# Squares of two tiles interleaved, samples scaled inside waits and half a product group moved ahead of the sample transposes, in the norms of a hybrid encoder step

## The chip, the cores and the metric

One core of a Trainium2 chip runs the whole kernel in one launch. The metric is device time in microseconds, the median of several runs.

## The reference

Two encoder layers over 256 prompt tokens (one sequence) and 8 x 16 sample tokens, 384 tokens in all, of width 1024. Every layer has three blocks, each closed by a gated residual, with RMSNorm before and after the block:

```
h = rms_norm(x, gains[0]) * (1 + sc1) + sh1
x = x + MACARON_W * ga1 * rms_norm(swiglu(h, w_f1_in, w_f1_out), gains[1])
h = rms_norm(x, gains[2]) * (1 + sc2) + sh2
y, rows = token_mixing(h, ...)
x = x + ga2 * rms_norm(y, gains[3])
h = rms_norm(x, gains[4]) * (1 + sc3) + sh3
x = x + MACARON_W * ga3 * rms_norm(swiglu(h, w_f2_in, w_f2_out), gains[5])
```

`rms_norm` divides a token's 1024 values by the root of their mean square plus 1e-6. Shift, scale and gate (`sh`, `sc`, `ga`) come from the condition of the sequence through `w_ada`, so all prompt tokens share theirs and every sample sequence has its own. Token mixing is one projection `h @ w_in` into three groups of heads (stick-breaking attention, gated linear attention, sparse attention with an indexer), joined by `w_out`. All is float32.

## The kernel before, in words

**Tiles.** The 384 tokens are three tiles of 128: the samples are tile 2, the prompt tiles 0 and 1. `TILES = (2, 0, 1)` is the order in which a norm takes them, so k = 0 is the samples, k = 1 is tile 0, k = 2 is tile 1. Between norms the activations lie transposed, feature by token, as `act_hi` and `act_lo` (the value split in a high part and a rest), eight chunks f of 128 features. Each weight unit of 128 x 2048 is loaded by SP, split by ACT (`w_hi`, the line of `split_hi`) and DVE (`w_lo`, L1282), and every product is three: hi x hi, lo x hi, hi x lo (L1926 to L1928 for projections into the block, L1973 to L1977 and L2007 to L2009 for projections back to tokens). Weights keep PE fed unit by unit; the first unit behind a norm is split ahead of it into `first_hi` and `first_lo`.

**A norm.** There are six, three a layer: `nth` 0 behind FFN 1, 1 behind the mixing, 2 behind FFN 2. The last one only updates x. In `last_two` PE ends the products of a projection tile by tile, the last unit half by half of the 1024 columns (`last_products`: six products of 512 columns for the left half, `y_left_done`, six for the right). For each tile ACT squares and sums the left and right half of y (`sum_y`: L920, L923, then Sqrt L927); DVE multiplies y with the gate (`gate_y`: mean L1371, left L1372, right L1374, reciprocal L1376) and updates x in two halves (L1379). Then the new x is normalised: ACT squares its halves (`sum_new_x`: L932, L935, Sqrt L939), DVE adds the left sum to eps for that Sqrt (`norm_new_x`: L1385), takes the reciprocal (L1387) and multiplies x by it in two halves (L1391, `x_left_normed`, `x_normed`). The order, written out by hand on both engines in `renorm`, is y0, x0, y1, y2, x1, x2.

**Back to features.** PE transposes the samples (`transpose_samples`, L1838) when the normalised samples are there, then does `last_products(2)` for tile 1, a group of products with `w_ada` (L1868, conditioning of later blocks, `ada_quarters`), the transposes of tile 0 and tile 1 (L1844), and, where `nth != 1`, a second group with `w_ada`. ACT applies scale and shift to the prompt chunks on their way out of PSUM (`modulate`: L914 to act_hi, L915 to y), DVE takes act_lo from them (`split_prompt`, L1305). The samples are handled by DVE alone: scale (L1250, whole width of 1024), shift (L1256), high part (L1298), low part (L1300) in `modulate_samples` and `split_samples`, and in front of FFN 2 (`nth` 1's norm) by halves of 512 columns (`scale_half` L1319, `shift_half` L1325, `high_half` L1330, `low_half` L1335). PE's first product of the next block (L1926) waits for act_lo of chunk 0, which stands behind these in DVE's queue.

**Key duplicates.** In the mixing, the 64 rows of the key of the sparse attention and of its indexer are needed on both halves of the partitions (`kc_dup`, `ki_dup`). PE makes them with `dup_eye`, a 64 x 128 matrix of two identities (L2130), ACT copies them from PSUM (L1017). The index products (L2152, L2153) read `ki_dup`.

Each engine runs its own instructions in the written order; semaphores tie them together. Loads of `w_ada` are issued by POOL when PE has used a slot, loads of other weights by SP when DVE has split a slot.

Of the kernel before, what the change touches and what calls it, by code (L numbers as in the profile page):

```python
# [26 lines left out]
P = 128  # L27
# [26 lines left out]
def encoder_program(nc, T):  # L54
# [93 lines left out]
    with ExitStack() as ctx:  # L148
# [37 lines left out]
        dup_eye = place("dup_eye", [P, P])  # L186
# [204 lines left out]
        dup_mm = sig("dup_mm", 2)  # L391
# [224 lines left out]
        def _(pool):  # L616
# [15 lines left out]
            for t, v in ((ones_v, 1.0 / DV), (causal, 0.0), (gla_mask, 1.0),  # L632
                         (restart, 1.0), (dup_eye, 0.0), (spread, 0.0), (sb_mask_c, 0.0), (head_rows, 0.0),
                         (other_seq, 0.0), (parity, 1.0), (ones_row, 1.0)):
                pool.memset(t[:], v)
# [9 lines left out]
            keep_where(dup_eye[0:64, :].rearrange("p (a n) -> p a n", a=2), [[0, 2], [-1, 64]], 0, 1, ALU.not_equal, 1.0)  # L645
# [194 lines left out]
        def _(act):  # L840
# [37 lines left out]
            for l in range(DEPTH):  # L878
# [38 lines left out]
                def sum_y(nth, k):  # L917
# [3 lines left out]
                                   accum_out=st(k, LEFT_SUM)).then_inc(y_left_squared.sem, 1)  # L921
                    wait_y(act, l, nth, k)
# [6 lines left out]
                def sum_new_x(nth, k):  # L929

                    act.wait_ge(x_left_ready.sem, x_left_ready.at(l, TT * nth + k + 1))
                    act.activation(square_out[:, 0:512], x[:, TILES[k], 0:512], ACT.Square, scale=float(D) ** -0.5,  # L932
                                   accum_out=st(k, X_LEFT_SUM)).then_inc(x_left_squared.sem, 1)
                    act.wait_ge(x_ready.sem, x_ready.at(l, TT * nth + k + 1))
# [6 lines left out]
                def renorm(nth):  # L941

                    if nth == 2 and l == LAST:
                        for k in range(TT):
                            sum_y(nth, k)
# [65 lines left out]
                def copy_kvi():  # L1011
# [191 lines left out]
        def _(dve):  # L1203
# [50 lines left out]
            def shift_samples(nth):  # L1254

                dve.tensor_tensor(samples_4d(own_tok[2]), samples_4d(own_tok[2]), per_seq(3 * (nth % 3)), ALU.add)  # L1256
                dve.drain()

# [19 lines left out]
            for l in range(DEPTH):  # L1278
# [10 lines left out]
                def modulate_samples(nth):  # L1289

                    if l > 0 or nth > 0:
                        scale_samples(3 * l + nth)
                    shift_samples(nth)

                def split_samples():

                    tok = own_tok[2].rearrange("p (f n) -> p f n", f=KD)
                    dve.tensor_copy(act_hi[:, :, NP:N], tok)  # L1298
                    dve.drain()
                    dve.tensor_tensor(act_lo[:, :, NP:N], tok, act_hi[:, :, NP:N].bitcast(F32), ALU.subtract)  # L1300

# [6 lines left out]
                def split_prompts(nth):  # L1308

                    for f in range(KD):  # L1310
                        split_prompt(nth, f)
# [26 lines left out]
                def split_all_by_halves(nth):  # L1338

                    shift_half(nth, 0)  # L1340
# [6 lines left out]
                    if nth == 0:  # L1347
# [1113 lines left out]
```

## Time and profile before

| | |
|---|---|
| timed, median of 3 runs | 1632.11 us (1631.75 to 1632.22) |
| the profiled execution | 1630.43 us, of which its span 1628.8 |
| PE busy | 1587.3 us (97%), 10214 matmuls |
| DVE busy | 814.3 us (50%) |
| ACT busy | 586.2 us (36%) |
| POOL busy | 151.7 us (9%) |
| mean granted TensorE clock | 0.994 of full speed |
| moved by DMA | 266.01 MB, mean 163 GB/s |

The span runs from the first to the last instruction of one execution. Busy shares are over all stages; for a norm one reads the timeline of that stretch: a row has the start (from the span's start), the duration, the engine, the line, the operation, output and inputs, the count, and in brackets how long the engine had been idle and what released it. Rows that merge several instructions have one start and the time of all of them. Instructions of one engine overlap by some hundredths of a microsecond to a few tenths, so distances between starts are the better measure of what one costs in a queue.

### The profile page before, as it was taken

Reading aid. Unit: us, or ns where it says so; the run is one execution under the profiler, and the core shown is the slowest. Engines: PE = TensorE matmul, PEld = TensorE weight load, DVE = VectorE, ACT = ScalarE, POOL = GpSimd, SP = SyncE. Lnnn points to the kernel's source line nnn. Section 1 sums busy time; section 2 is a strip of 40 time slices with the busy share of each in tenths; the row PEclk is TensorE's granted clock in tenths of the full one; section 3 lists DMA queues with packets and bytes.
Section 4 is the critical chain, followed back from the end, with each engine's and each line's share of the span. In section 5 each row is a group of like instructions: output and inputs, shape, how many; then the busy total and the mean of one; then the engine's idle time right before and its main releaser. Section 6 shows DMA issues by size and latency. Waiting matters only on the chain.

```text
span 1628.8 us, 26038 instructions
## 1 busy us (share of the span) xinstructions
PE 1587.3 (97%) x10214; PEld 1448.3 (89%) x10214; DVE 814.3 (50%) x1202; ACT 586.2 (36%) x816; POOL 151.7 (9%) x227
## 2 busy tenths in 40 slices
PE   5999999999999999999999999999999999999998
PEld 4999998879998799998879999987899879999987
DVE  3434442458658733443364444326675685444424
ACT  4322222363455522222262222224535644222222
POOL 5000000010242000000010000000105310000000
PEclk9999999999999999999999999999999999999999
DMA  9777744753345577444557744355534273444432
GB/s 346 232 232 214 233 128 155 229 147 104 104 134 191 148 233 231 123 121 152 185 176 228 233 129 129 129 181 181 143 106 128 83 233 104 128 125 119 135 119 84
DMA packets 254150, 266.01 MB, mean 163 GB/s; under 512 B 11727, under 2 KB 216653, under 8 KB 254066
## 3 DMA queue, kind: packets, MB, share of 16 engines
q1 hardware_dynamic: 231968, 183.52, 37.7%
q0 software_dynamic: 22080, 81.26, 14.4%
q8 instruction: 61, 1.00, 0.3%
q14 instruction: 23, 0.19, 0.0%
q10 hardware_dynamic: 18, 0.04, 0.0%
HBM read 258.70 MB, written 6.09 MB: 163 GB/s over the span
## 4 chain that ended last, share of the span: by engine, by line
PE 90%; DVE 5%; ACT 2%; DMA 1%; DVEq 1%; issue 1%; SPq 0%; ACTq 0%
PE ps L1926 20%; PE ps L1928 19%; PE ps L1927 19%; PE ps L1973 7%; PE ps L1975 7%; PE ps L1977 7%; PE ps L1868 2%; DMA w_ada_g<-in_w_ada_dram 1%; PE ps L2009 1%; PE ps L2007 1%; PE ps L2008 1%; DVE x L1379 1%; PE ps L1990 1%; PE ps L2264 0%; PE ps L2137 0%
## 5 line engine op out<-in xcount | busy, mean ns | idle before, releaser
L1926 PE MATMUL ps<-act_hi,w_hi 128*128 128x384 f32 x1696 | 572.6, 338 | 0.4 <-DVE w_lo L1282 0.4
L1928 PE MATMUL ps<-act_hi,w_lo 128*128 128x384 f32 x1696 | 567.1, 334 | 0.0
L1927 PE MATMUL ps<-act_lo,w_hi 128*128 128x384 f32 x1696 | 566.8, 334 | 0.0
L1282 DVE TENSOR_TENSOR w_lo<-w_raw,w_hi 128x2048 fp32r<-128x2048 f32 x158 | 363.7, 2302 | 238.2 <-ACT w_hi L898 207.6
L1926 PEld LDWEIGHTS ps<-act_hi,w_hi 128*128 128x128 f32 x1696 | 318.4, 188 | 10.8 <-issue 9.9
L898 ACT ACTIVATE w_hi<-w_raw 128x2048 fp32r<-128x2048 f32 x128 | 245.4, 1917 | 227.6 <-PE ps L1977 226.8
L1927 PEld LDWEIGHTS ps<-act_lo,w_hi 128*128 128x128 f32 x1696 | 318.5, 188 | 0.0
L1928 PEld LDWEIGHTS ps<-act_hi,w_lo 128*128 128x128 f32 x1696 | 318.3, 188 | 0.0
L962 ACT ACTIVATE silu_g<-ps 128x384 f32<-128x384 f32 x88 | 43.3, 492 | 546.7 <-PE ps L1928 546.7
L1422 DVE TENSOR_TENSOR hid_f<-silu_g,ps 128x384 f32<-128x384 f32 x88 | 48.8, 554 | 375.4 <-ACT silu_g L962 375.4
L1973 PE MATMUL ps<-w_hi,hid_hi 128*128 128x512 f32 x480 | 148.6, 391 | 0.0
L1975 PE MATMUL ps<-w_hi,hid_lo 128*128 128x512 f32 x480 | 147.9, 389 | 0.0
L1977 PE MATMUL ps<-w_lo,hid_hi 128*128 128x512 f32 x480 | 147.9, 389 | 0.0
L1977 PEld LDWEIGHTS ps<-w_lo,hid_hi 128*128 128x128 f32 x480 | 90.1, 188 | 18.9
L1975 PEld LDWEIGHTS ps<-w_hi,hid_lo 128*128 128x128 f32 x480 | 90.1, 188 | 18.9
L1973 PEld LDWEIGHTS ps<-w_hi,hid_hi 128*128 128x128 f32 x480 | 89.4, 188 | 17.9
L702 POOL DMA_DIRECT2D w_ada_g<-in_w_ada_dram x16 | 11.7, 734 | 495.8 <-PE ps L1977 495.8
L885 ACT ACTIVATE w_hi<-w_raw 128x2048 fp32r<-128x2048 f32 x30 | 57.5, 1915 | 0.0
L1428 DVE TENSOR_TENSOR hid_lo<-hid_f,hid_hi 128x384 f32 (+1 forms) x88 | 49.1, 558 | 10.9 <-issue 0.2
L712 POOL DMA_DIRECT2D w_ada_sb<-in_w_ada_dram x32 | 23.0, 719 | 263.3 <-PE ps L1868 259.1
L1868 PE MATMUL ps<-w_ada_sb,silu_cT 128*32 128x256 f32 x752 | 45.7, 382 | 0.0
L1519 DVE COPY U<-ps 128x384 f32<-128x384 f32 x24 | 13.4, 558 | 57.5 <-PE ps L1928 57.2
(421 smaller groups left out, 1555.1 us busy)
## 6 DMA issues: line engine op xcount, KB each, us to landing
w_raw<-in_w_ffn_in_dram SPq DMA_DIRECT2D x176, 512.0 KB, 5.1
w_ada_sb<-in_w_ada_dram POOLq DMA_DIRECT2D x45, 1024.0 KB, 7.1
w_raw<-in_w_ffn_out_dram SPq DMA_DIRECT2D x88, 512.0 KB, 4.1
w_raw<-in_w_in_dram SPq DMA_DIRECT2D x46, 512.0 KB, 4.7
w_ada_g<-in_w_ada_dram POOLq DMA_DIRECT2D x16, 1024.0 KB, 5.4
w_raw<-in_w_out_dram SPq DMA_DIRECT2D x16, 512.0 KB, 4.7
w_ada_g<-in_w_ada_dram SPq DMA_DIRECT2D x5, 1024.0 KB, 15.8
w_ada_s<-in_w_ada_dram POOLq DMA_DIRECT2D x3, 1024.0 KB, 10.9
```

The source lines that it names most:

```text
L885: act.activation(w_hi[slot][:], w_raw[slot][:], ACT.Copy).then_inc(hi_ready.sem, 1)
L898: act.activation(w_hi[slot][:], w_raw[slot][:], ACT.Copy).then_inc(hi_ready.sem, 1)
L1282: dve.tensor_tensor(w_lo[slot][:], w_raw[slot][:], w_hi[slot][:].bitcast(F32), ALU.subtract).then_inc(lo_ready.sem, 1)
L1422: dve.tensor_tensor(hid_f32[:], silu_g[:, s % 2, :], ps[:, IN_BANK[s % 2] + 1, 0:N], ALU.mult)
L1428: dve.tensor_tensor(hid_lo[:, chunk, :], one, hid_hi[:, chunk, :].bitcast(F32), ALU.subtract).then_inc(hidden_ready.sem, 1)
L1868: m = pe.matmul(ps[32 * g:32 * g + 32, bank, 0:256], silu_cT[:, 2 * q + k, :], w_ada_slot[slot][:, k, 256 * g:256 * g + 256], start=(q + k ...
L1926: pe.matmul(out, w, a, start=first, stop=False)
L1927: pe.matmul(out, w, al, start=False, stop=False)
L1928: return pe.matmul(out, wl, a, start=False, stop=last)
L1973: pe.matmul(y_half(tile, half), a, w_hi[slot][:, cols[half]], start=first, stop=False)
L1975: pe.matmul(y_half(tile, half), al, w_hi[slot][:, cols[half]], start=False, stop=False)
L1977: m = pe.matmul(y_half(tile, half), a, w_lo[slot][:, cols[half]], start=False, stop=last)
```

## The change

1. ACT's `sum_y` and `sum_new_x` are cut into `square_y_left`, `square_y_right`, `square_x_left`, `square_x_right`. For tiles 0 and 1 the order becomes y1, left y2, left x1, (drain), right y2, right x1, x2, with the left square of x1 written into the other half of `square_out`.
2. DVE's `gate_y` and `norm_new_x` are cut the same way; the order for the two prompt tiles becomes y1, left gate of y2, the left half of the samples' scale, right gate of y2, mean of x1, update of x by y2, normalise x1 left, mean of x2, x1 right, x2.
3. The samples are scaled, shifted and split by halves behind every norm (`split_by_halves`), the left half of the scale inside `renorm`, the right half at the start of `split_by_halves` (for `nth` 2 where it was).
4. On PE the left half of `last_products(2)` stands ahead of the sample transposes.
5. The key duplicates are copied by ACT from U, in two halves of 64 partitions each; `dup_eye`, its products and their semaphore go.

In the diff `split_first` holds what `split_all_by_halves(0)` did for the first block.

```diff
-                    sum_y(nth, 0)
-                    sum_new_x(nth, 0)
-                    sum_y(nth, 1)
-                    sum_y(nth, 2)
-                    sum_new_x(nth, 1)
-                    sum_new_x(nth, 2)
+                    square_y_left(nth, 0)
+                    square_y_right(nth, 0)
+                    square_x_left(nth, 0)
+                    square_x_right(nth, 0)
+                    square_y_left(nth, 1)
+                    square_y_right(nth, 1)
+                    square_y_left(nth, 2)
+                    square_x_left(nth, 1, square_out[:, 512:1024])
+                    act.drain()
+                    square_y_right(nth, 2)
+                    square_x_right(nth, 1)
+                    square_x_left(nth, 2)
+                    square_x_right(nth, 2)
...
-                    for n, dst in ((1, ki_dup), (0, kc_dup)):
-                        act.wait_ge(dup_mm.sem, dup_mm.at(l, n + 1))
-                        act.activation(dst[:], ps[:, 6 + n, 0:N], ACT.Copy).then_inc(dup_ready.sem, 1)
+                    for dst, tile in ((ki_dup, KI), (kc_dup, KV)):
+                        for rows in (slice(0, 64), slice(64, 128)):
+                            ins = act.activation(dst[rows, :], U[0:64, tile, :], ACT.Copy)
+                        ins.then_inc(dup_ready.sem, 1)
...
-                def scale_half(nth, a):
-
-                    dve.wait_ge(sample_tr.sem, sample_tr.at(0, 3 * l + nth))
+                def scale_half(norm, a):
+
+                    banks = SAMPLE_BANKS_F2 if norm % 3 == 2 else SAMPLE_BANKS
+                    dve.wait_ge(sample_tr.sem, sample_tr.at(0, norm))
                     four = lambda t: t.rearrange("p (f b t) -> p f b t", f=KD // 2, t=S)
-                    dve.tensor_tensor(four(half_tok(a)), four(ps[:, SAMPLE_BANKS_F2[a], :]), per_seq(3 * nth + 1)[:, half_of(a)], ALU.mult)
+                    dve.tensor_tensor(four(half_tok(a)), four(ps[:, banks[a], :]), per_seq(3 * (norm % 3) + 1)[:, half_of(a)], ALU.mult)
                     dve.drain()
...
+                def split_by_halves(nth):
+
+                    if nth != 2:
+                        scale_half(3 * l + nth, 1)
                     shift_half(nth, 0)
                     high_half(0)
                     low_half(0)
                     split_prompt(nth, 0)
                     if nth == 2:
-                        scale_half(nth, 1)
+                        scale_half(3 * l + nth, 1)
                     split_prompt(nth, 1)
...
                     gate_y(nth, 0)
-                    norm_new_x(nth, 0)
+                    new_x_mean(nth, 0)
+                    new_x_rstd(nth, 0)
+                    normalise(0, x_left_normed, left)
+                    normalise(0, x_normed, right)
                     gate_y(nth, 1)
-                    gate_y(nth, 2)
-                    norm_new_x(nth, 1)
-                    norm_new_x(nth, 2)
+                    gate_left(nth, 2)
+                    scale_half(3 * l + nth + 1, 0)
+                    gate_right(nth, 2)
+                    new_x_mean(nth, 1)
+                    add_y(nth, 2)
+                    new_x_rstd(nth, 1)
+                    normalise(1, x_left_normed, left)
+                    new_x_mean(nth, 2)
+                    normalise(1, x_normed, right)
+                    new_x_rstd(nth, 2)
+                    normalise(2, x_left_normed, left)
+                    normalise(2, x_normed, right)
...
-                    modulate_samples(0)
-                    split_samples()
-                    split_prompts(0)
+                    split_by_halves(0)
...
-                scale_half(2, 0)
-                split_all_by_halves(2)
+                split_by_halves(2)
...
-                    def last_products(k):
+                    def last_products(k, halves=range(2)):
                         tok, slot = slice(TILES[k] * P, (TILES[k] + 1) * P), (u + 1) % 2
-                        for half in range(2):
+                        for half in halves:
...
+                    last_products(2, (0,))
                     pe.wait_ge(gate_read.sem, gate_read.at(l, 2 * nth + 2))
                     banks = SAMPLE_BANKS_F2 if nth == 1 else SAMPLE_BANKS
                     pe.wait_ge(x_left_normed.sem, x_left_normed.at(l, TT * nth + 1))
                     transpose_samples(banks, range(4))
                     pe.wait_ge(x_normed.sem, x_normed.at(l, TT * nth + 1))
                     transpose_samples(banks, range(4, KD)).then_inc(sample_tr.sem, 1)
-                    last_products(2).then_inc(unit_used.sem, 1)
+                    last_products(2, (1,)).then_inc(unit_used.sem, 1)
...
-                    for n, tile in enumerate((KV, KI)):
-                        pe.matmul(ps[:, 6 + n, 0:N], dup_eye[0:64, :], U[0:64, tile, :], start=True, stop=True).then_inc(dup_mm.sem, 1)
```

## Rows read from the trace of the kernel before

**Rows 1.** PE's waits: who waited <- for whom: us, times, longest us

```profile
PE ps L1926 <- DVE act_lo L1305: 7.2, 6, 2.4
```

**Rows 2.** Timeline near 330 us, PE: start us, us, engine, line, operation

```profile
328.00 1.06 PE L1838 MATMUL ps<-ident,gate_tok 128*128 128x128 f32 x8 [0.67 <-DVE gate_tok L1391]
...
338.64 2.80 PE L1868 MATMUL ps<-w_ada_g,silu_cT 128*32 128x256 f32 x48
...
341.25 1.05 PE L1868 MATMUL ps<-w_ada_sb,silu_cT 128*32 128x256 f32 x16
...
342.94 0.41 PE L1926 MATMUL ps<-act_hi,first_hi 128*128 128x384 f32 x1 [0.64 <-DVE act_lo L1305]
...
351.34 0.38 PE L1882 MATMUL ps<-ident,ada_rows 128*128 128x128 f32 x2
```

**Rows 3.** Timeline near 330 us, DVE and ACT

```profile
329.65 1.41 DVE L1379 SCALAR_TENSOR_TENSOR x<-spare_tok,stat,x 128x512 f32<-128x512 f32 x2
...
331.21 0.15 DVE L1371 TENSOR_SCALAR stat<-stat 128x1 f32<-128x1 f32 x1
...
332.57 0.69 DVE L1374 TENSOR_TENSOR gate_tok<-ps,gate_tok 128x512 f32<-128x512 f32 x1 [0.61 <-ACT square_out L923]
...
333.18 0.15 DVE L1376 RECIPROCAL stat<-stat 128x1 f32<-128x1 f32 x1
...
333.40 1.41 DVE L1379 SCALAR_TENSOR_TENSOR x<-gate_tok,stat,x 128x512 f32<-128x512 f32 x2
...
334.74 0.15 DVE L1385 TENSOR_SCALAR small<-small 128x1 f32<-128x1 f32 x1
...
335.49 0.88 DVE L1391 TENSOR_SCALAR spare_tok<-x,stat 128x512 f32<-128x512 f32 x2
...
336.51 0.29 ACT L939 ACTIVATE stat<-stat,small 128x1 f32<-128x1 f32 x1
...
337.07 0.88 DVE L1391 TENSOR_SCALAR gate_tok<-x,stat 128x512 f32<-128x512 f32 x2
```

**Rows 4.** Timeline of the second kind of norm, layer 0

```profile
539.51 1.42 DVE L1379 SCALAR_TENSOR_TENSOR x<-gate_tok,stat,x 128x512 f32<-128x512 f32 x2
...
543.18 0.88 DVE L1391 TENSOR_SCALAR gate_tok<-x,stat 128x512 f32<-128x512 f32 x2
...
543.98 0.68 DVE L1319 TENSOR_TENSOR gate_tok<-ps,mod 128x512 f32<-128x512 f32 x1
...
544.74 0.69 DVE L1325 TENSOR_TENSOR gate_tok<-gate_tok,mod 128x512 f32<-128x512 f32 x1
...
547.18 0.41 PE L1926 MATMUL ps<-act_hi,first_hi 128*128 128x384 f32 x1 [2.37 <-DVE act_lo L1305]
```

**Rows 5.** Windows: stretch, length, busy by engine (instructions), granted clock, DMA share, GB/s

```profile
547.47:550.88 3.41, 3.41 (x13) 3.41 (x12) 3.18 (x8) 3.41 (x9) 0.00 (x0) 0.51 0.36 145
```

**Rows 6.** Timeline ahead of the second unit, layers 0 and 1

```profile
553.50 2.29 DVE L1282 TENSOR_TENSOR w_lo<-w_raw,w_hi 128x2048 fp32r<-128x2048 f32 x1 [1.37 <-ACT w_hi L898]
...
557.78 0.43 PE L1926 MATMUL ps<-act_hi,w_hi 128*128 128x384 f32 x1
...
1353.13 2.29 DVE L1282 TENSOR_TENSOR w_lo<-w_raw,w_hi 128x2048 fp32r<-128x2048 f32 x1 [1.38 <-ACT w_hi L898]
...
1356.66 0.42 PE L1926 MATMUL ps<-act_hi,w_hi 128*128 128x384 f32 x1
```

**Rows 7.** Timeline around the key duplicates

```profile
366.73 1.55 PE L2130 MATMUL ps<-U,dup_eye 64*128 64x384 f32 x4
...
368.21 0.44 PE L1926 MATMUL ps<-act_hi,w_hi 128*128 128x384 f32 x1
...
368.71 0.48 ACT L1017 ACTIVATE kc_dup<-ps 128x384 f32<-128x384 f32 x1
...
372.70 0.49 ACT L1000 ACTIVATE U<-ps 128x384 f32<-128x384 f32 x1 [3.50 <-PE ps L1928]
...
376.75 0.50 PE L2152 MATMUL ps<-ki_dup,U 64*128 64x128 f32 x4
```

More of the change, by code:

```diff
@@ L632, in _ @@
             for t, v in ((ones_v, 1.0 / DV), (causal, 0.0), (gla_mask, 1.0),
-                         (restart, 1.0), (dup_eye, 0.0), (spread, 0.0), (sb_mask_c, 0.0), (head_rows, 0.0),
+                         (restart, 1.0), (spread, 0.0), (sb_mask_c, 0.0), (head_rows, 0.0),
                          (other_seq, 0.0), (parity, 1.0), (ones_row, 1.0)):
@@ L927, in sum_y, with square_x_left, square_x_right @@
                     act.activation(st(k, Y_STD), st(k, RIGHT_SUM), ACT.Sqrt, bias=st(k, LEFT_MEAN)).then_inc(y_std.sem, 1)
-                def sum_new_x(nth, k):
+                def square_x_left(nth, k, out=square_out[:, 0:512]):
                     act.wait_ge(x_left_ready.sem, x_left_ready.at(l, TT * nth + k + 1))
-                    act.activation(square_out[:, 0:512], x[:, TILES[k], 0:512], ACT.Square, scale=float(D) ** -0.5,
+                    act.activation(out, x[:, TILES[k], 0:512], ACT.Square, scale=float(D) ** -0.5,
                                    accum_out=st(k, X_LEFT_SUM)).then_inc(x_left_squared.sem, 1)
+                def square_x_right(nth, k):
                     act.wait_ge(x_ready.sem, x_ready.at(l, TT * nth + k + 1))
@@ L1336, in low_half, with split_first @@
                                       act_hi[:, half_of(a), NP:N].bitcast(F32), ALU.subtract)
-                def split_all_by_halves(nth):
+                def split_first():
+                    shift_half(0, 0)
+                    high_half(0)
+                    low_half(0)
+                    for f in range(4):
+                        split_prompt(0, f)
+                    dve.wait_ge(ada_tr, 2)
+                    add_shift_half(1)
+                    shift_half(0, 1)
+                    high_half(1)
+                    low_half(1)
+                    for f in range(4, KD):
+                        split_prompt(0, f)
+                def split_by_halves(nth):
+                    if nth != 2:
+                        scale_half(3 * l + nth, 1)
                     shift_half(nth, 0)
@@ L1380, in gate_y, with new_x_mean, new_x_rstd @@
                                                  in1=x[:, tile, cols], op0=ALU.mult, op1=ALU.add).then_inc(ready.sem, 1)
-                def norm_new_x(nth, k):
+                def gate_y(nth, k):
+                    gate_left(nth, k)
+                    gate_right(nth, k)
+                    add_y(nth, k)
+                def new_x_mean(nth, k):
                     dve.wait_ge(x_left_squared.sem, x_left_squared.at(l, TT * nth + k + 1))
                     dve.tensor_scalar(st(k, X_LEFT_MEAN), st(k, X_LEFT_SUM), EPS, None, ALU.add).then_inc(x_left_mean.sem, 1)
+                def new_x_rstd(nth, k):
                     dve.wait_ge(x_std.sem, x_std.at(l, TT * nth + k + 1))
@@ L1388, in norm_new_x, with normalise @@
                     dve.drain()
+                def normalise(k, normed, cols):
                     tile = TILES[k]
-                    for normed, cols in ((x_left_normed, slice(0, 512)), (x_normed, slice(512, 1024))):
-                        dve.tensor_scalar(own_tok[tile][:, cols], x[:, tile, cols], st(k, X_RSTD), None, ALU.mult).then_inc(normed.sem, 1)
+                    dve.tensor_scalar(own_tok[tile][:, cols], x[:, tile, cols], st(k, X_RSTD), None, ALU.mult).then_inc(normed.sem, 1)
                 def renorm(nth):
+                    left, right = slice(0, 512), slice(512, 1024)
                     if nth == 2 and l == LAST:
@@ L1485, in _ @@
                 if l == 0:
-                    split_all_by_halves(0)
+                    split_first()
                 else:
-                    modulate_samples(0)
-                    split_samples()
-                    split_prompts(0)
+                    split_by_halves(0)
                 n0, component, groups = N_F1[l], LOOP_F1[l][1], LOOP_F1[l][2]
```

50 lines of the change are left out of this document (12 added, 38 removed).

## The prediction

> **What bounds the kernel now.** I read the page first: PE is busy 1587.3 of 1628.8 us, so only what takes work off PE or closes one of its gaps can show. The waits of PE name the gaps that this change is near [rows 1]: the first product after a norm waits for DVE's act_lo (six times, 7.2 us in all, the longest 2.4); sample and prompt transposes wait for the normalised rows too, under 1 us each time. Then I read the timeline of one norm of each kind. There are five norms with a next product: three with a second group of ada products behind the transposes (near 312, 816 and 1113 us; the same steps at the same distances) and two without (near 525 and 1325 us). In the first kind PE stands 0.67 us before the sample transposes, goes through tile 1's transposes to the second ada group at 338.64, ends it at 341.25 + 1.05 = 342.30, and starts its first product at 342.94 [rows 2]. In the second kind nothing stands between the transposes and the first product, so PE waits for DVE's queue: norm of tile 1 at 543.18, scale at 543.98, shift at 544.74, product at 547.18 [rows 4]. So the norm chain on ACT and DVE is the limit there. The sweep of windows shows one thing more: in both second-kind norms the granted clock is 0.5, PE's lower level of 1.2 GHz, while the first products run (one stretch of the two stands in [rows 5]; the other begins at 1346.2); before each fall PE had done only transposes and stood idle.
>
> **Norms of the first kind, three of them.** *The sample transposes after half a product group.* PE no longer stands before them: six products (0.23 us each, 1.4 in all) run first, and rows that came at 328.00 are there by 328.5 [rows 2]. It saves the 0.67, and the left half of tile 1 is ready that much and the 0.8 to 1.1 of the transposes earlier. So gate_left, which started at 331.21 [rows 3] when ACT's square came, now waits only for DVE itself.
> *DVE's queue.* I lay it out from the unchanged start of tile 0's x at 329.65, with pitches from [rows 3]: a pair of x updates 1.34 (333.40 to 334.74), gate with its mean 0.67 (0.07 for the small one that starts at 331.21, the multiply 0.61, from 332.57 to 333.18), reciprocal with drain 0.22 (333.18 to 333.40). Pair to 330.99, gate_left to 331.66, scale_half(0) with drain 0.76 (the pitch of the same form, 543.98 to 544.74) to 332.42, gate_right 0.61 to 333.03 (its square, before at 332.57, is earlier, so it doesn't bind), mean and reciprocal to 333.31: tile 1's x update starts 0.09 earlier than the 333.40 of before, although a scale has been put ahead of it. Then the gain comes: before, ACT's Sqrt for tile 0 waited for a mean that stood behind the pair; now mean and square lie before it. Tile 0 normalises at 333.31 + 1.34 + 0.24 = 334.89 instead of 335.49. For tile 1: ACT starts the right square when the pair has ended (+1.50, the pair's 1.41 and a handoff), square and sum take some 0.8 (an estimate from the 0.6 and 0.2 that the timeline shows for them), and 0.56 lies from Sqrt to normalise (336.51 to 337.07): 336.15 instead of 337.07, 0.92 earlier.
> *Where it ends on PE.* Tile 1's transposes and the second ada group follow by 0.92 and end at 341.38. DVE meanwhile: normalise to 336.95 (0.80), scale_half(1) to 337.71, then 2.44 from the start of a half-width shift to the product, as in [rows 4]: 340.15. Before, whole-width scale, shift, high and low kept PE until 342.94. So PE is now bound by its own ada group and starts at 341.38: 1.56 earlier. Next late is nothing: the next unit's w_lo moves by the 0.92 of ACT and had over a microsecond in hand. Three times 1.56 is 4.7 us.
>
> **Norms of the second kind, two of them.** PE never waited for samples there, so the right half of tile 1 comes at the old time, and gate_right too. The mean put behind it costs 0.07: x update at 539.58. By the same steps as above tile 1 normalises 0.8 earlier (1.50 + 0.8 + 0.56 after the start: 542.4 for 543.18 [rows 4]). Behind it the scale (0.76) is gone, moved into the wait for the right square, which was 0.6 long (the 0.61 of [rows 3] repeats here). So shift starts where scale did, at 543.98 - 0.8 = 543.2, and the product 2.44 later at 545.64: 1.54 earlier.
> *The clock.* The first unit took 351.34 - 342.94 = 8.40 us at full clock [rows 2]; with the fall, 557.78 - 547.18 = 10.60 [rows 4, 6] with 0.6 of small turns before unit 1 in it, so a fall costs up to 1.6. From the last ada product to the first main product the way is 1.5 us shorter, and everything moves by 3 us in layer 0 and some 10 in layer 1 against the places where it fell. I take it that both falls go. But then unit 1 is late: its w_lo begins at 553.50 and ends at 555.79, moves only with ACT's modulate, by 0.8, and is there at 555.1 with 0.1 of handoff, while PE would be there at 545.64 + 8.40 + 0.6 = 554.6. So unit 1 starts at 555.1 for 557.78 [rows 6], a gain of 2.7 of which 0.5 is given back in a new wait; in layer 1 at 1354.7 (1353.13 + 2.29 - 0.8 + 0.1) for 1356.66, 1.9. Both together 4.6 us; with the falls left in place 2 x 1.54 = 3.1.
> The Trainium skill (TensorE: Matmul & The Clock Gate, Part 4) says that transposes don't count as activity of PE for its clock. The trace agrees as far as it goes: the falls come behind transposes and idle time that the page counts as busy in part. The same page (Part 1) says that how many matmuls run slow varies from run to run of one kernel with where they fall; by that rule both falls could stay or move, and the sum would be 10.8 in place of 12.3, which is rival 1. Which of the two holds here the trace of one execution can't show.
>
> **Key duplicates.** PE loses the products with dup_eye: from 366.73 to the next product at 368.21 are 1.48 us [rows 7], in a stretch where PE waits for nobody; two layers, 2.96 us. ACT gets four copies of 64 rows instead of two of 128. The trace has no ACT copy from one half of the partitions to the other. Below: nothing gained, since the old copies of 0.48 [rows 7] lay beside PE; above: no row. I take 0.5 each, like those nearest rows. They begin about a microsecond before the old ones' end at 368.71 [rows 7], at 367.7; PE wants them at 375.3 (the index product of 376.75 less 1.48), so even 1.9 us each is hidden. Behind them on ACT stands the copy of unit 2, which waited 3.50 for PE. At DVE the sums of the decays pass only part of the 1.48 on, but it waits for PE again in the units behind. Removing dup_eye's memset and mask on POOL lies at the start, where nobody waits for it: nothing. split_first and the last norm keep their order: nothing.
> *Moved waits.* DVE's scale_half(0) waits for sample_tr with gate_right and tile 1's x behind it; PE raises it at 328.5 + 0.9 = 329.4, DVE asks at 331.7 (in the second kind the distance is longer still). ACT's drain stands before a square that waits for PE anyway. The extra means (0.07) are counted. No DMA changes queue; POOL's ada loads come earlier with PE.
>
> **The sum.** 2.96 + 4.7 + 4.6 = 12.3 us. The profiled execution took 1630.43 (span 1628.8 and 1.6 around it) and would take 1618.1. It lies 1.7 below the median of the timed runs, 1632.11; the same 12.3 from that gives 1619.8, my forecast.
>
> **Rivals.**
> 1. *The clock falls as often as before*, at other places. For it: what decides lies partly outside the order of work, since one of the two falls begins after the first product and the other before it. Gain 2.96 + 4.7 + 3.1 = 10.8: 1621.3. Falls in plenty (two more) would give 1624.4.
> 2. *DVE's queue becomes the bound.* In the first kind it has no idle time in my layout from 329.65 to 335.75, so each uncounted tenth (a drain, a handoff, in eight instructions a norm) is paid: 0.8 a norm, 4 us: gain 8.3, 1623.8. Against it: the pitches come from the same instructions.
> 3. *A fall more goes*, as one near 500 us in layer 0 could, and the execution is like the profiled one: 12.3 + 1.6 + 1.7: 1616.5.
> 4. *The norms give nothing*, because PE waits at another step for what it no longer waits for here, and only the key duplicates count: 1629.1, within 0.2%.
> 5. *Slower: ACT's copies across the partitions.* From 1.9 us each they hold PE's index products, and from (7.6 + 6.2) / 4 = 3.45 each they eat the whole gain. At 4 us: 2 x (16 - 7.6) - 12.3 = 4.5 slower, 1636.6. For it only that no row shows such a copy.
>
> **How the numbers follow.** Forecast 0.40, rival 1 0.25, rival 2 0.20, rival 3 0.06, rival 4 0.05, rival 5 0.04. The range 1616.2 to 1625.0 takes in the first four with a fall more or less at either end and leaves out the last two. A measurement can tell about 0.2% (3.3 us) from no change: faster 0.91, within 0.05, slower 0.04.
>
> **What would show it.** No PE wait before the sample transposes; tile 1 normalised 0.9 and 0.8 us earlier against the end of the product group; the first product of the first kind directly behind the ada group; PE waiting 0.5 to 0.9 us for w_lo before unit 1 of the second kind, and clock 1.00 there; the product behind unit 2's transposes 1.48 earlier, ACT's copies near 0.5. It is wrong if the copies are over 1.9, if the normalise of tile 0 doesn't come before 335.2 on the old scale, or if the clock falls in the first kind.

## The result, and the profile after

| | before | after |
|---|---|---|
| median of the timed runs | 1632.16 us (1631.75 to 1633.46) | 1620.95 us (1617.44 to 1621.48) |
| ratio | | 0.9933, 95% interval [0.9921, 0.9945] |
| profiled execution | 1630.43 us (span 1628.8) | 1621.48 us (span 1619.7) |
| mean granted clock of it | 0.994 | 0.992 |

The change is 11.2 us faster; 12.3 were forecast (1619.8 for 1620.95), well inside the range. But the profiled span is only 9.1 us shorter. To see where, I cut both spans at instructions that both kernels have: the first x update of each norm, the first product behind it, and the late part of the key duplicates (ACT's last copies into kc_dup in each layer, near 490 and 1290 us). Stage by stage, minus the same stage of before, us (worked out from the timelines):

```
stage                            before  after  forecast
start to norm 1                  324.56  +1.38   0
norm 1 (first kind)               18.38  -1.69  -1.56
layer 0, up to the late keys     146.72  -1.67  -1.48
layer 0, mixing                   40.79   0.00   0
norm 2 (second kind)              16.73  -1.57  -1.54
behind it, to norm 3             280.53  -1.17  -1.16
norm 3 (first kind)               18.40  -1.70  -1.56
behind it, to norm 4             278.79  +0.03   0
norm 4 (first kind)               18.39  -1.70  -1.56
layer 1, up to the late keys     146.93  -1.53  -1.48
layer 1, mixing                   39.85  +2.48   0
norm 5 (second kind)              16.73  -1.57  -1.54
behind it, to the last norm      270.96  -0.41  -0.36
```

The changed stages give 13.0 us, 0.7 more than forecast. Two stages in which no work of PE was changed, the start (only `dup_eye`'s memset and mask on POOL went there) and the mixing of layer 1, take 3.9 back. The waits of PE (who waited <- for whom: us in total, times, longest):

```profile
PE ps L1948 <- DVE act_lo L1299: 4.7, 4, 1.6
PE ps L1866 <- DVE spare_tok L1405: 2.9, 5, 0.9
PE ps L1860 <- DVE gate_tok L1230: 2.2, 1, 2.2
PE ps L1918 <- DMA w_ada_g<-in_w_ada_dram: 2.2, 2, 1.6
...
PE ps L1948 <- DVE w_lo L1289: 1.0, 2, 0.6
```

The wait for act_lo fell from 7.2 to 4.7 us and from 2.4 to 1.6 at the longest [rows 1]; of the four waits left, two are in the start (0.9 and 0.6) and two in the norms of the second kind (1.6 each), so those of the first kind have none. L1860, the sample transposes, waits only once, in the start. Of the two waits for w_lo the one of 0.4 in the start was there before; the other, 0.57 near 1347 us, is new. A norm of the first kind, DVE's timeline (start us, us, engine, line, operation; everything stands 1.38 us later than in before, from the start):

```profile
331.03 1.41 DVE L1382 SCALAR_TENSOR_TENSOR x<-spare_tok,stat,x 128x512 f32<-128x512 f32 x2
332.36 0.14 DVE L1366 TENSOR_SCALAR stat<-stat 128x1 f32<-128x1 f32 x1
332.42 0.68 DVE L1367 TENSOR_TENSOR gate_tok<-ps,gate_tok 128x512 f32<-128x512 f32 x1
333.02 0.68 DVE L1309 TENSOR_TENSOR gate_tok<-ps,mod 128x512 f32<-128x512 f32 x1
333.78 0.69 DVE L1373 TENSOR_TENSOR gate_tok<-ps,gate_tok 128x512 f32<-128x512 f32 x1
...
334.67 1.41 DVE L1382 SCALAR_TENSOR_TENSOR x<-gate_tok,stat,x 128x512 f32<-128x512 f32 x2
336.00 0.16 DVE L1399 RECIPROCAL stat<-stat 128x1 f32<-128x1 f32 x1
336.23 0.48 DVE L1405 TENSOR_SCALAR spare_tok<-x,stat 128x512 f32<-128x512 f32 x1
...
337.48 0.88 DVE L1405 TENSOR_SCALAR gate_tok<-x,stat 128x512 f32<-128x512 f32 x2
```

No row has an idle time before it: the queue is closed, as it was laid out. The same norm on PE:

```profile
329.91 1.03 PE L1860 MATMUL ps<-ident,gate_tok 128*128 128x128 f32 x8
...
336.78 1.12 PE L1866 MATMUL ps<-ident,spare_tok 128*128 128x128 f32 x8 [0.87 <-DVE spare_tok L1405]
338.02 1.09 PE L1866 MATMUL ps<-ident,gate_tok 128*128 128x128 f32 x8
339.04 2.80 PE L1890 MATMUL ps<-w_ada_g,silu_cT 128*32 128x256 f32 x48
341.65 1.05 PE L1890 MATMUL ps<-w_ada_sb,silu_cT 128*32 128x256 f32 x16
342.63 0.44 PE L1948 MATMUL ps<-act_hi,first_hi 128*128 128x384 f32 x1
```

The sample transposes come without a wait, and the first product stands directly behind the ada group. The 0.87 us ahead of the prompt transposes is the place where DVE still holds PE. In a norm of the second kind the product waits for DVE alone, 1.59 where it was 2.4:

```profile
540.94 1.09 PE L1866 MATMUL ps<-ident,gate_tok 128*128 128x128 f32 x8
543.63 0.41 PE L1948 MATMUL ps<-act_hi,first_hi 128*128 128x384 f32 x1 [1.59 <-DVE act_lo L1299]
...
1347.53 0.44 PE L1948 MATMUL ps<-act_hi,w_hi 128*128 128x384 f32 x1 [0.57 <-DVE w_lo L1289]
```

The last row is the first product of the second unit in layer 1. In layer 0 the trace puts only 0.10 us ahead of the same product, at 553.06.

The sweep of windows (columns: busy us and instructions of each engine, then PE's granted clock, the share of DMA, GB/s) has full clock in the first units behind both second-kind norms, and the lower level, 1.2 GHz, in the mixing stages. Before fell near 500 us too, and the mixing stage of layer 0 has the same length in both; the fall near 1290 is new.

```profile
core 0: us, PE busy (x) PEld busy (x) DVE busy (x) ACT busy (x) POOL busy (x), PEclk, DMA share, GB/s
495.00:498.00 3.00, 3.00 (x52) 2.96 (x56) 2.34 (x2) 2.59 (x4) 0.00 (x0) 1.00 0.00 0
498.00:501.40 3.40, 3.40 (x61) 2.68 (x46) 3.35 (x7) 0.46 (x2) 0.00 (x0) 0.51 0.26 57
1290.00:1296.70 6.70, 6.70 (x79) 5.53 (x79) 6.39 (x16) 0.98 (x3) 0.00 (x0) 0.50 0.45 112
543.63:552.00 8.37, 8.37 (x48) 8.16 (x48) 6.08 (x12) 8.35 (x15) 0.00 (x0) 1.00 0.38 155
1338.09:1346.00 7.91, 7.91 (x45) 7.77 (x46) 5.62 (x12) 7.89 (x15) 0.00 (x0) 1.00 0.01 2
```

My theory at this point: the terms of the sum stand, and the rest is the clock, whose falls move between executions. Rivals: the 0.67 us of the samples and the order of the squares are worth little each and the gain comes from elsewhere in the norm; the 3.9 us are a cost of the change. The ratios below are to runs of the kernel before that were timed with each experiment (medians 1631.35 to 1631.79 us). The runs are read by the same stages, since a fall adds or takes 1 to 2.5 us of a whole span, as much as most of the edits.

### The profile page after: what moved, and what is told of

The parts are those of the page before. It is cut to its first block, busy times and chain, and to the rows that moved or that the text cites. A ratio compares the mean times of both kernels' runs of the same rounds, so it can differ in the third digit from the quotient of the medians.

```text
span 1619.7 us, 26048 instructions
## 1 busy us (share of the span) xinstructions
PE 1585.0 (98%) x10206; PEld 1447.2 (89%) x10206; DVE 813.8 (50%) x1214; ACT 589.4 (36%) x820; POOL 150.7 (9%) x225
## 4 chain that ended last, share of the span: by engine, by line
PE 90%; DVE 4%; ACT 3%; DMA 1%; DVEq 1%; issue 1%; SPq 0%; ACTq 0%
PE ps L1948 19%; PE ps L1950 19%; PE ps L1949 19%; PE ps L1995 8%; PE ps L1997 8%; PE ps L1999 8%; PE ps L1890 3%; DMA w_ada_g<-in_w_ada_dram 1%; PE ps L2285 1%; DVE x L1382 1%; PE ps L2012 1%; PE ps L2031 1%; PE ps L2029 1%; PE ps L2030 1%; ACT y L912 1%
## 5 line engine op out<-in xcount | busy, mean ns | idle before, releaser
L1948 PEld LDWEIGHTS ps<-act_hi,w_hi 128*128 128x128 f32 x1696 | 318.3, 188 | 10.8 <-issue 8.8
## 6 DMA issues: line engine op xcount, KB each, us to landing
w_ada_s<-in_w_ada_dram POOLq DMA_DIRECT2D x3, 1024.0 KB, 10.8
```

What stands on the lines that cost most here:

```text
L1948: pe.matmul(out, w, a, start=first, stop=False)
```

## The experiments

**The key duplicates alone**, on the kernel before (the lines of the diff for ki_dup, kc_dup and dup_eye, nothing else).

> The kernel before with the change of the key duplicates alone. My theory: the term stands by itself, 1.48 to 1.67 us in each of two layers, all of it between the last transposes of the keys and the next product of PE (2.2 us apart before, 0.6 to 0.75 now): 2.96 to 3.3 us less than before, ratio 0.9980 to 0.9982; everything else of the trace keeps its distances. Rival: the 1.67 seen in the changed kernel belongs to the norms (buffers free earlier), then about 0 here. Falls of the clock can add or take 1.7 to 3.4 us of the total, so the stage decides.

Measured: 1628.73 us, ratio 0.9983 [0.9973, 0.9992]. The two stages up to the late keys are 1.68 and 1.71 us shorter, every norm is within 0.02 of before. In each pair of ACT's copies the first stays on partitions 0 to 63 and the second goes to 64 to 127; they cost the same:

```profile
368.60 1.05 ACT L1014 ACTIVATE ki_dup<-U 64x384 f32<-64x384 f32 x2
369.68 1.06 ACT L1014 ACTIVATE kc_dup<-U 64x384 f32<-64x384 f32 x2
```

One by one they took 0.516 and 0.523 us (ki_dup), 0.525 and 0.525 (kc_dup). The term stands by itself.

**PE's old order**, on the changed kernel.

```diff
-                    last_products(2, (0,))
                     pe.wait_ge(gate_read.sem, gate_read.at(l, 2 * nth + 2))
...
-                    last_products(2, (1,)).then_inc(unit_used.sem, 1)
+                    last_products(2).then_inc(unit_used.sem, 1)
```

> The changed kernel with PE's old order: the sample transposes stand ahead of the whole last product group of the third tile. Forecast's reading (the half group saves the 0.67 us that PE stood there): PE stands 0.6 to 0.7 again in each of five norms, 3.2 us slower than the changed kernel. My theory now: in the changed kernel PE stands 0.87 us ahead of the next transposes of a norm of the first kind, so the 0.67 only moves there; what is paid is the later start of gate_left on DVE (0.2 to 0.3 in each of five norms), 1.0 to 1.5 us slower than the changed kernel in all, gain against before 7.6 to 8.1 on the scale on which the changed kernel has 9.1.

Measured: 1619.91 us, 0.9926 [0.9908, 0.9944]; the whole can't be told from the changed kernel, the stages can. The wait of 0.67 is back ahead of the sample transposes, but the one ahead of tile 0's prompt transposes shrinks from 0.87 to 0.23:

```profile
329.18 1.06 PE L1860 MATMUL ps<-ident,gate_tok 128*128 128x128 f32 x8 [0.67 <-DVE gate_tok L1405]
...
336.81 1.11 PE L1866 MATMUL ps<-ident,spare_tok 128*128 128x128 f32 x8 [0.23 <-DVE spare_tok L1405]
```

Norms 1 and 3 gain 1.45 and 1.47 instead of 1.69 and 1.70, norms 2 and 5 1.51 for 1.57. So the half group is worth 0.24 in the first kind, not 0.67. Norm 4 lost 1.03, more than expected: besides the 0.24, its ada products stood 0.57 us (0.76 by the distance of starts) for weights that came by DMA, a wait that the changed kernel doesn't have there. Why the weights came late was not tested.

```profile
1135.60 1.07 PE L1890 MATMUL ps<-w_ada_sb,silu_cT 128*32 128x256 f32 x16 [0.57 <-DMA w_ada_sb<-in_w_ada_dram]
```

**The left half of the samples scaled after the normalisation**, on the changed kernel (scale_half(..., 0) taken out of renorm and put at the head of split_by_halves).

> The changed kernel with the left half of the samples scaled after the normalisation again, not in DVE's wait for the right square. If the wait covers it as the forecast says: second kind 0.76 us later at the first product in each of two norms (1.5 in all); in the first kind the normalisation keeps its time and PE, bound by its own ada group, starts when it did: 0. If the wait does not cover it in the first kind (there the right square is there early, since half a product group ran ahead): the second x update and everything behind it on PE come up to 0.7 us earlier in each of three norms (2.1 faster), so the total lies between 1.5 slower and 0.6 faster than the changed kernel.

Measured: 1620.61 us, 0.9932 [0.9913, 0.9950]. Second kind: 0.81 and 0.80 instead of 1.57, so the wait covers the whole scale there (0.76). First kind: norms 1 and 3 gain 2.12 and 2.14, 0.43 more than the changed kernel; norm 4 0.05 more, since DVE paused 0.45 us in it for nothing that the profile shows. The row that tells why:

```profile
332.10 0.68 DVE L1368 TENSOR_TENSOR gate_tok<-ps,gate_tok 128x512 f32<-128x512 f32 x1
333.02 0.69 DVE L1374 TENSOR_TENSOR gate_tok<-ps,gate_tok 128x512 f32<-128x512 f32 x1 [0.24 <-ACT square_out L923]
```

With the half group ahead, the right square is late by 0.24 only; a scale of 0.76 put in that wait costs 0.5 of it. The clock fell in this execution near 545 and 1337 us, behind both second-kind norms.

**The squares in their old order**, on the changed kernel.

```diff
                     square_y_left(nth, 2)
-                    square_x_left(nth, 1, square_out[:, 512:1024])
-                    act.drain()
                     square_y_right(nth, 2)
+                    square_x_left(nth, 1)
                     square_x_right(nth, 1)
...
                     gate_right(nth, 2)
+                    add_y(nth, 2)
                     new_x_mean(nth, 1)
-                    add_y(nth, 2)
                     new_x_rstd(nth, 1)
                     normalise(1, x_left_normed, left)
+                    normalise(1, x_normed, right)
                     new_x_mean(nth, 2)
-                    normalise(1, x_normed, right)
```

> The changed kernel with the squares and means in their old order (both squares of y, then both of x; the mean of the second tile behind the third tile's x updates), the scale still in the wait and PE's new order kept. My theory: the second tile's normalisation waits for its mean again, 0.6 us later, the third tile's 0.6 to 0.9 later, and this is paid in full in each of five norms: 3 to 4.5 us slower than the changed kernel. Rival (the order of the squares is worth little, the gain of the norms comes from the scale and the half group): under 1 us slower.

Measured: 1623.74 us, 0.9947 [0.9927, 0.9966]. Norms 1, 2, 4 and 5 gain 0.88, 0.77, 0.88 and 0.78: 0.8 less each. DVE waits for both square roots again, and PE's wait ahead of the prompt transposes grows from 0.87 to 1.32. The same two rows of the kernel before, and then those of this run:

```profile
335.25 0.16 DVE L1387 RECIPROCAL stat<-stat 128x1 f32<-128x1 f32 x1 [0.36 <-ACT stat L939]
...
336.83 0.16 DVE L1387 RECIPROCAL stat<-stat 128x1 f32<-128x1 f32 x1 [0.40 <-ACT stat L939]
```

```profile
336.12 0.16 DVE L1398 RECIPROCAL stat<-stat 128x1 f32<-128x1 f32 x1 [0.36 <-ACT stat L942]
...
337.70 0.16 DVE L1398 RECIPROCAL stat<-stat 128x1 f32<-128x1 f32 x1 [0.40 <-ACT stat L942]
```

Norm 3 was 0.72 longer than before here: the clock fell in it (839 to 842 us). Four norms of 0.8 measured and norm 3 taken to be like them make 4.0 us, the largest single part of the change that was undone here.

**Each key copy four times**, on the changed kernel (a drain and a loop of four round the activation).

> The changed kernel with each of ACT's four copies of the key duplicates done four times. At 0.52 us each, as the trace of the changed kernel has them, that is 12 more copies or 6.3 us a layer. The forecast put the room at four copies of 1.9 us (7.6 us), so 16 x 0.52 = 8.3 us would hold PE's index products by 0.7 at most, 1.5 us in two layers. My theory: less than that, since ACT also stood idle behind the copies: 0 to 1.5 us slower than the changed kernel, seen between the transposes of the keys and the late duplicates of the stage. Rival (there is no such room, ACT's queue is near the path): 6 us a layer, 12 us slower, slower than the kernel before.

Measured: 1625.13 us, 0.9964 [0.9950, 0.9978]. With the drain one copy takes 0.59, all sixteen 9.4, and PE does wait:

```profile
366.10 4.68 ACT L1030 ACTIVATE ki_dup<-U 64x384 f32<-64x384 f32 x8
370.86 4.66 ACT L1030 ACTIVATE kc_dup<-U 64x384 f32<-64x384 f32 x8
...
375.66 0.50 PE L2175 MATMUL ps<-ki_dup,U 64*128 64x128 f32 x4 [2.20 <-ACT kc_dup L1030]
```

PE would have come at 375.66 - 2.20 = 373.46, 7.4 us after the copies began: a room of 1.84 us for each of four, where the forecast had 1.9. The stages grew by 3.8 and 3.1, more than the 2.2 of the wait. In layer 0 the clock fell right behind it (near 377 us); in layer 1 PE waits 0.6 us more for a w_lo near 1180 us, which it doesn't in the changed kernel. I did not part the rest. My bound of 1.5 for both layers was too low: the drains, left out of it, make the copies some 1.1 us a layer longer (9.4 for 8.3), and what came behind the wait was not in it at all. The rival's 12 is out: the two stages grew by 7.0 together.

**Dense products in PE's idle time**, on the kernel before.

```diff
                     if nth != 1:
                         ada_quarters(n + 1, range(4), ADA_BANK_B)
+                    else:
+                        split_ready(U_F2IN)
+                        for again in range(12):
+                            pe.matmul(ps[:, 5, 0:N], first_hi[:, 0:P], first_lo[:, 0:N], start=True, stop=True)
```

> The kernel before with twelve dense products more (of the first unit's two parts, into a bank that nobody reads) in PE's idle time before the first product of each norm of the second kind. They take some 2.1 us, PE is free for 2.4 there, so the first product keeps its time. If the falls of the clock come from PE standing idle behind transposes there, both go (layer 0: 1.6 less; layer 1: 1.2 less; total 2.4 to 2.9 us less than before on the stage from that product to the next norm). If the falls have another cause, there is still one near 547 or 1346 us, and the total is that of before.

Measured: 1629.77 us, 0.9991 [0.9981, 1.0]. Both falls are gone, and the stages behind the two norms are 1.53 and 1.17 shorter: 2.7 us, on the old norm's own timing. The twelve products took 2.36 us, and the first product kept its time within 0.2.

```profile
544.00:552.00 8.00, 7.25 (x45) 6.58 (x44) 7.14 (x16) 6.64 (x16) 0.39 (x1) 1.00 0.71 262
1340.00:1350.00 10.00, 8.63 (x67) 7.30 (x59) 8.64 (x21) 8.13 (x21) 0.00 (x0) 1.00 0.00 0
```

The timed median moved by 1.6 only, which fits falls that are not in every execution. This is one profile: in the three others with the old norms a fall was missing in one of six places without any filler, so that both are gone here speaks for the idle time as their cause, and doesn't prove it.

**Wide products in the stretch of value products**, on the changed kernel: the first chunk of the output projection for one tile (six products of 512 columns in the trace, where the expectation says twelve) moved up.

```diff
+                        if b == 5 and between is not None:
+                            between()
...
-                    for kc in range(2):
+                    for kc in range(1 if tile == 0 else 0, 2):
```

> The changed kernel with twelve dense products of the output projection (first chunk of the first tile) moved up into the stretch of small value products in which the clock fell near 498 us and 1290 us. The products only change places, so without any effect on the clock: within 0.3 us of the changed kernel in both mixing stages. If the fall follows from the long stretch of narrow products: no fall there in either layer, 0 to 1.7 us less in layer 0 and 2.5 less in layer 1 than the profile of the changed kernel. If the falls keep to their places, the small products were not their cause.

Measured: 1618.74 us, 0.9923 [0.9906, 0.9940]. Clock 1.00 through both mixing stages; they are 0.64 shorter and 2.13 shorter than in the profile of the changed kernel:

```profile
495.00:503.00 8.00, 8.00 (x107) 7.01 (x107) 7.03 (x13) 2.99 (x4) 0.00 (x0) 1.00 0.30 90
1285.00:1300.00 15.00, 14.46 (x137) 12.06 (x136) 12.61 (x22) 5.88 (x9) 3.44 (x5) 1.00 0.25 83
```

But a mixing stage without a fall is 0.98 shorter than before in layer 0 where the products were left in their place (the duplicates alone, the dense products in idle time), so the move itself costs 0.35 there, and some 0.4 in layer 1 by the same comparison (+0.35 against -0.05 in two kernels without a fall). Falls: none in two places here, where most kernels have one. Since mixing stages without a fall occur with the stretch unbroken too, two places alone don't show that the move prevents them.

**The second unit's high part ahead of the modulation**, on the changed kernel.

```diff
                 renorm(1)
+                split_hi(U_F2IN + 1, (U_F2IN + 1) % 2)
                 modulate(2)
```

> The changed kernel with ACT's high part of the second unit made ahead of ACT's modulation in the norms of the second kind (1.92 to 2.01 us of work put where ACT stood idle for 1.35). Forecast's step: unit 1 waits 0.6 us for its low part, which waits for this high part; then the wait goes and unit 1 begins 0.6 us earlier in each of two norms, 1.2 us less than the changed kernel in all. Rival: the modulation comes 0.6 us later and holds the first unit's own products (its low parts behind the modulation), so the 0.6 is paid there instead: 0.

Measured: 1619.27 us, 0.9932 [0.9915, 0.9949]. The stages behind the second-kind norms are 0.38 and 0.87 shorter than in the changed kernel, 1.25 in all; the norms themselves keep their 1.57. ACT's modulation begins at 540.51; in the changed kernel it was 541.48, which is 540.14 on this one's scale (all stands 1.34 us earlier here). It comes 0.37 late and holds nobody:

```profile
538.70 1.90 ACT L882 ACTIVATE w_hi<-w_raw 128x2048 fp32r<-128x2048 f32 x1
540.51 0.54 ACT L911 ACTIVATE act_hi<-ps,mod 128x256 fp32r<-128x256 f32 x1
```

**These together.** With the wide products, and then without them.

> Three things that the runs so far point to, together, on the changed kernel: the left half of the samples scaled in the wait only in the norms of the second kind (0.43 in each norm of the first kind where the scale was taken out, 0.05 in the one where DVE paused: 0.9 to 1.3 in all), the second unit's high part ahead of the modulation (1.25), and the dense products in the stretch of value products (no fall there: 0.6 in layer 0 and 2.1 in layer 1 of the profile). If they add: stages of the norms -2.1, first stage behind the second kind -1.5 and less, no fall near 498 and 1290 us, 2.2 us less than that kernel without the first two, some 4 less than the changed kernel in the median: ratio to before 0.991. If they share a cover (an earlier first product finds ada weights or the unit's parts late), less than 1.2 of the 2.2 is seen.

> The same without the moved dense products: only the scale per kind of norm and the high part ahead. By the sum 0.9 to 1.3 and 1.25 less than the changed kernel, 2.2 to 2.5 in all; falls of the clock in the mixing stages as there, in some executions. If e9 and this one agree in their timed runs, the falls in mixing are worth nothing in the median.

Measured: 1618.06 us, 0.9913 [0.9900, 0.9927], and 1617.31 us, 0.9908 [0.9893, 0.9924]. Both keep the gains of the parts: norms of the first kind 2.12, 2.14 and 1.75, the stage behind norm 5 1.28 and 1.24 shorter than before. The two agree in their runs, so breaking the stretch of value products is worth nothing that can be told. That the falls which it spares are paid for by the 0.75 us of the move and by the executions without a fall is my reading; no run parts the two. The kernel without them is the fastest measured here, some 3.6 us under the changed kernel by the medians, though the two intervals overlap a little.

In both, the clock fell behind norm 2, which it had not done in the changed kernel, and that stage is as long as before (-0.03 and -0.06): a fall costs 1.5 us there once the wait for w_lo is gone.

**Both kernels once more**, for the clock.

> The changed kernel once more, for where its clock falls. If the falls are set by the order of work alone (as the forecast has it for the second-kind norms), they stand where they stood: two of them long at the start, one near 498 us, two near 1290 us, none in a norm of the second kind. If their places vary from execution to execution (rival 1), at least one of these moves or goes, with 1.2 to 1.7 us of the span.

> The kernel before once more, for the same question. Set by the order of work: falls near 500, 547 and 1346 us again and none in layer 1's mixing, span 1628.8. Varying: at least one of these is missing or another has come, span 1.2 to 1.7 us off for each; every stage without a fall in either has the same length within 0.1 us.

Measured: the changed kernel fell at the same three places (start, 498, 1290 us; span 1620.1, all stages within 0.13 us). The kernel before did not: its span was 1633.6, 4.8 us more, with no fall near 500, a longer one at 547, one near 1301 and one near 1353:

```profile
500.00:503.00 3.00, 3.00 (x79) 2.75 (x79) 2.34 (x2) 1.80 (x3) 0.00 (x0) 1.00 0.00 0
547.20:554.00 6.80, 6.00 (x19) 6.04 (x20) 5.50 (x13) 6.80 (x13) 0.00 (x0) 0.50 0.35 143
1301.60:1308.30 6.70, 6.70 (x79) 5.53 (x79) 6.38 (x16) 1.00 (x3) 0.00 (x0) 0.50 0.42 114
1352.80:1356.10 3.30, 3.30 (x12) 3.30 (x11) 3.13 (x9) 3.30 (x8) 0.00 (x0) 0.50 0.01 2
```

Layer 1's mixing took +2.51 there, as it took +2.48 in the changed kernel. The 2.5 us are therefore no cost of the change. Nor are the 1.38 of the start: two kernels with all of the change in them (each copy four times, the high part ahead) had the start of before within 0.05 us, with a fall there as short as its; where the start was 1.0 to 2.4 us longer (the unchanged kernel again among them, 1.78), the clock was low for longer.

## Why the prediction was right, and where it was lucky

**Key duplicates**: 1.68 and 1.71 against 1.48. The small miss: I took the distance from 366.73 to 368.21 [rows 7] and counted the six transposes ahead of it at their 0.75. With the unit's products directly behind them they take 0.57. The copies (forecast 0.5, measured 0.52) and the room (forecast 1.9, measured 1.84) held; rival 5 is out.

**First kind**: 1.70 against 1.56, by the steps named. On the old scale x update at 333.29 (forecast 333.31), tile 0 normalised at 334.85 (334.89; the one whose mean and square were put first), the next tile at 336.10 (336.15), the first product directly behind the ada group at 341.25 (341.38). What was wrong is a step that the sum didn't need: "It saves the 0.67". By itself the half group saves 0.24, since PE stands ahead of the next transposes in its stead. What the norm gains is the order of the squares (0.8 of 1.7) and, with it, the split in halves behind it: the wait of 0.64 ahead of the first product [rows 2] is gone. That the halves did this is argued, since they were not undone by themselves here. The scale in the wait takes 0.43 back. The forecast saw that DVE's queue had no idle time, and priced it only as a risk; that was the place of a further gain. Rival 2 is thus right on the mechanism, wrong on the price: no uncounted tenths came.

**Second kind**: 1.57 to the first product against 1.54. On the old scale tile 1 was normalised at 542.38 (forecast 542.4, though its own terms, 539.58 + 1.50 + 0.8 + 0.56, make 542.44, a gain of 0.74 and not 0.8) and the first shift began at 543.18 (543.2). Behind it 1.17 and 0.41 against 1.16 and 0.36 (2.7 and 1.9 less 1.54). The wait for w_lo, forecast at 0.5 in layer 0 and up to 0.9 in layer 1, stands in the trace with 0.10 and 0.57. Making the high part ahead took 0.38 and 0.87 off the two stages, so the late part cost nearly what was forecast, though only part of that shows as a wait for w_lo. The price of the two falls stood the test of the dense products (1.53 and 1.17, forecast up to 1.6 each, without any change of order). Their going did only in part: over all profiles of this study, a fall stood behind a second-kind norm in 5 of 6 places with the old order of the norm and no filler, and in 5 of 20 with the new.

**The clock elsewhere**: missed, and here rival 1 told it better. What the norms lost in falls, the mixing stages seem to have taken up: without the wide products, 3 of 8 mixing stages had a fall with the old norms (the filler's kernel among them), 13 of 16 with the new. Leaving out the start and the end of the span, the three profiles with old norms had the low clock for 10.2, 17.1 and 10.2 us, the eight with new norms and no wide products for 6.8 to 13.7, 10.2 in the mean. So the falls moved more than they went, and the gain by rival 1, 10.8 us, and by the forecast, 12.3, lie on both sides of the measured 11.2. Three profiles against eight don't settle how many fewer there are. That the median came within 1.1 us of the forecast is in part luck: the changed stages gave 0.7 more than forecast, falls that no term of the sum had took 3.9 back in the profile, and how the falls lay in the other timed executions no trace shows.

The Trainium skill (TensorE: Matmul & The Clock Gate, Part 1) says of the matmuls at a kernel's start that how many run slow varies from run to run of one kernel. The two profiles of the kernel before agree, at the start and in the middle of the span too: 4.8 us of span apart with no instruction changed, 1.8 of it in the start. The changed kernel fell at the same places twice. One profile is one draw: that of before was a good one (1.7 us under its median), that of after a poor one (0.5 over), and by this the spans differ by 9.1 and the medians by 11.2.

**Rivals 3 and 4**: the norms gave what they should, so 4 is out. A fall fewer near 500 us (rival 3) did come in some profiles (the kernel before when it was run again, the duplicates alone, the dense products, the last combination), with 0.98 us and not 1.6, but not in the changed kernel's two profiles.

## What to carry to other kernels

Cut two traces at instructions that both have and compare stage by stage; with a clock that draws anew in each execution, the stage tells an edit of 0.2 us where the whole can't tell 2. An operation put in a wait is free only as long as that wait is, and another part of the same change may have shortened it: check each pair of edits, and by kind of place (here the same line paid 0.76 in two norms and cost 0.43 in two others). A wait ahead of an instruction is worth only what the next wait on that engine doesn't take over.

## What the runs showed of the hardware

An ACT copy of 64 x 384 from partitions 0 to 63 to 64 to 127 took 0.52 to 0.53 us, as the same copy within partitions 0 to 63 beside it did; the old copies of 128 x 384 from PSUM took 0.48 to 0.49. PE's clock fell to its lower level while PE was busy throughout: in mixing it had done 3.65 us of value products with 32 columns before the fall near 498 us, with no wait, so a fall here doesn't need idle time. The same stretch ran without a fall in four other profiles, so it doesn't settle it alone either. With six products of 512 columns in its middle no mixing stage fell, four of four, which is few. Rows of the changed kernel ahead of that fall:

```profile
493.15 1.03 PE L2279 MATMUL ps<-sq,TM 128*128 128x256 f32 x4
494.01 3.65 PE L2285 MATMUL ps<-sb_swT,va_past 128*128 128x32 f32 x32
497.60 1.67 PE L2340 MATMUL ps<-TM,k_rows 32*64 32x128 f32 x64
```

DVE paused 0.45 us between two instructions with nothing to wait for, ahead of the same x update of norm 4 in the three kernels with the scale taken out of the wait (0.45 in each); why stays open.
